# A conditioned decoder trunk on one core: which of w_ada's first groups are cut in two, in which order they load, and how the input projection begins

## What is computed

```python
sc = silu(c)                                  # 1 prompt row and 8 sampled rows
mod = sc @ w_ada + b_ada                      # w_ada (1024, 6144)
sh1, s1, g1, sh2, s2, g2 = split(mod, 6)
h = rmsnorm(x, norm1_g) * (1 + s1) + sh1      # shift sh1, scale s1
z = h @ w_in                                  # w_in (1024, 6144)
# z feeds three mixers (convolution, pooling, short convolution), gates, and w_o;
# then x + g1 * mixed, a second norm with sh2 and s2, 16 experts of which 2 serve a token, a last norm
```

## Time and profile before

| | before |
|---|---|
| median of 3 runs | 872.23 us |
| lowest, highest | 871.78, 873.41 us |
| profiled execution: span | 871.9 us |
| PE, PEld busy | 839.9, 701.3 us (96%, 80%) |
| DVE, ACT busy | 683.7, 465.4 us (78%, 53%) |
| chain that ended last | PE 82%, DVE 8%, DMA 3%, ACT 2% |
| mean granted TensorE clock | 0.987 |

### The profile page before, as it was taken

The page is one execution under the profiler, slowest core; times in us unless marked ns, Lnnn a source line. Parts: engine busy times, 40 slices in busy tenths (PEclk is TensorE's granted clock), DMA queues, the critical chain, the costliest instruction groups (busy, mean ns, idle before and its releaser), DMA issues.

```text
span 871.9 us, 14906 instructions
## 1 busy us (share of the span) xinstructions
PE 839.9 (96%) x5047; PEld 701.3 (80%) x5047; DVE 683.7 (78%) x939; ACT 465.4 (53%) x556; POOL 76.7 (9%) x71
## 2 busy tenths in 40 slices
PE   7899999999999999999999989999999999999994
PEld 2489999989899999899777457888888888887851
DVE  0781638978798678499438889999989999899888
ACT  4652442343422221642222457888888888888852
POOL 0002000000000000230000002000100001003750
PEclk9989999999999999999999999999999999999998
DMA  9858535354543231123671479988895899999962
GB/s 328 277 174 290 194 127 169 121 169 150 159 154 108 89 96 50 42 87 123 211 276 74 170 252 398 400 327 310 316 400 217 317 398 400 400 400 397 366 197 98
DMA packets 90997, 201.24 MB, mean 231 GB/s; under 512 B 8792, under 2 KB 13400, under 8 KB 90918
## 3 DMA queue, kind: packets, MB, share of 16 engines
q1 hardware_dynamic: 78813, 165.25, 53.4%
q0 software_dynamic: 5136, 18.42, 5.9%
q10 hardware_dynamic: 7003, 16.95, 5.3%
HBM read 182.97 MB, written 18.35 MB: 231 GB/s over the span
## 4 chain that ended last, share of the span: by engine, by line
PE 82%; DVE 8%; DMA 3%; ACT 2%; issue 2%; SPq 1%; ACTq 1%; POOL 0%; POOLq 0%; DVEq 0%
PE ps L804 31%; PE ps L655 12%; PE ps L657 12%; PE ps L656 12%; PE ps L884 3%; DVE w_lo L1590 2%; PE ps L999 2%; DMA region_a<-in_x_prompt_dram 2%; PE ps L836 2%; PE ps L1121 1%; PE ps L683 1%; ACT w_hi L1146 1%; PE ps L684 1%; DMA region_b<-h_rows,slot_idx 1%; PE ps L1034 1%
## 5 line engine op out<-in xcount | busy, mean ns | idle before, releaser
L1590 DVE TENSOR_TENSOR w_lo<-raw,w_hi 128x1024 fp32r<-128x1024 f32 x202 | 241.6, 1225 | 100.1 <-ACT w_hi L1146 98.0
L1146 ACT ACTIVATE w_hi<-raw 128x1024 fp32r<-128x1024 f32 x202 | 207.8, 1056 | 198.2 <-PE ps L804 150.6
L655 PE MATMUL ps<-w_hi,hT_hi 128*128 128x512 f32 (+1 forms) x512 | 205.5, 401 | 3.6 <-DVE w_lo L1590 1.4
L657 PE MATMUL ps<-w_hi,hT_lo 128*128 128x512 f32 (+1 forms) x512 | 202.1, 395 | 0.0
L656 PE MATMUL ps<-w_lo,hT_hi 128*128 128x512 f32 (+1 forms) x512 | 201.5, 394 | 0.0
L804 PE MATMUL ps<-hT_hi,w_hi 128*128 128x260 f32 x768 | 156.6, 285 | 1.7 <-DVE w_lo L1590 0.9
L804 PE MATMUL ps<-hT_lo,w_hi 128*128 128x260 f32 x768 | 155.1, 283 | 0.0
L804 PE MATMUL ps<-hT_hi,w_lo 128*128 128x260 f32 x768 | 155.0, 283 | 0.0
L804 PEld LDWEIGHTS ps<-hT_hi,w_hi 128*128 128x128 f32 x768 | 119.1, 190 | 5.0 <-DVE w_lo L1590 3.9
L804 PEld LDWEIGHTS ps<-hT_lo,w_hi 128*128 128x128 f32 x768 | 119.5, 190 | 0.0
L804 PEld LDWEIGHTS ps<-hT_hi,w_lo 128*128 128x128 f32 x768 | 118.9, 189 | 0.0
(11 more groups left out here) (332 smaller groups left out, 840.3 us busy)
## 6 DMA issues: line engine op xcount, KB each, us to landing
raw<-in_exp_w_dram SPq DMA_DIRECT2D x96, 512.0 KB
region_a<-in_exp_w_dram SPq DMA_DIRECT2D x80, 512.0 KB
raw<-in_w_in_dram SPq DMA_DIRECT2D x48, 512.0 KB
raw<-in_w_ada_dram SPq DMA_DIRECT2D x30, 512.0 KB
expert_rows<-region_b ACTq DMA_DIRECT2D x17, 512.0 KB, 6.4
region_b<-in_exp_w_dram SPq DMA_DIRECT2D x16, 512.0 KB
region_b<-in_w_ada_dram SPq DMA_DIRECT2D x14, 512.0 KB, 9.0
expert_rows<-region_a POOLq DMA_DIRECT2D x8, 512.0 KB, 8.3
```

The lines of the kernel that those rows point to most:

```text
L655: pe.matmul(out, pairs[0], moving[0], start=start, stop=False)
L657: return pe.matmul(out, pairs[1], moving[0], start=False, stop=stop)
L1146: act.activation(w_hi[:, split_slot(n), :], place, ACT.Copy).then_inc(hi_done, 1)
L1590: return dve.tensor_tensor(out, whole, first.bitcast(F32), ALU.subtract)
```

## The change

The roles of w_ada's first four groups are exchanged: the shift groups 0 and 1 become the split ones and load first, the scale groups 2 and 3 the native ones, and they load behind x, the last four of their quarters behind the first two quarters of z group 0. PE no longer runs the natives first: it runs the eight split quarters, turns parameters and both shift groups, 16 identity transposes, and then sets native quarters between the blocks of x. z group 0 is cut into parts of one quarter and one tile: tiles 0 to 2 of quarter 0 come first, then two native quarters, tiles 0 to 2 of quarter 1, then tile 3 of both. On ACT all eight hi cuts stand ahead of the squares, and ACT multiplies two of x's four tiles by the norm itself, with a `scale` operand. On DVE the shift is finished before the norm. The core of the diff:

```diff
-ITEMS = [("a", g) for g in range(G_NAT, G_HEAD)] + [("z", 0), ("z", 1)]
+ITEMS = [("a", g) for g in range(G_SPLIT)] + [("z", 0), ("z", 1)]
...
 # SP
-            for h in range(6):
-                native(h)
+            for n in range(N_HEAD):
+                quarter(n)
             sp.dma_start(x_in[0:ND, 4, :], ...)
             for i in range(NP // P):
                 sp.dma_start(x_in[:, i, :], ...)
-            for h in range(6, 4 * G_NAT):
+            for h in range(4):
                 native(h)
-            for n in range(N_MIX):
-                if n == N_HEAD + 4:
+            for n in range(N_HEAD, N_MIX):
+                if n == N_HEAD + 2:
+                    for h in range(4, N_NAT):
+                        native(h)
+                elif n == N_HEAD + RAW:
                     for dst, src in state_loads:
...
-                elif n == N_HEAD + RAW:
-                    sp.wait_ge(ssq_ready, NTILE)
+                elif n == N_HEAD + RAW + 2:
+                    sp.wait_ge(hT_lo_done, KD + 2)
                     sp.wait_ge(turned, 2)
...
 # PE
+            pe.wait_ge(cT_split, 2)
+            for n in range(4):
+                ada_quarter(n, 4)
+            for n in range(4, 8):
+                ada_quarter(n, 7)
+            turn_params()
+            pe.wait_ge(fold_ready, 1)
+            turn_mod(0, 0, 0)
+            turn_mod(1, 0, 36).then_inc(modT_done, 1)
+            head_running(16)
+            native_quarter(0)
+            native_quarter(1)
+            pe.wait_ge(xn_ready, NTILE)
+            for p, b in ((0, 2), (1, 3), (2, 4)):
+                turn_x(p, b)
+            native_quarter(2)
+            native_quarter(3)
+            for k in range(3, KD):
+                if k >= 4:
+                    pe.wait_ge(xT_out, k - 3)
+                turn_x(k, X_BANK[k])
+            turn_sampled()
+            native_quarter(4)
+            turn_mod(2, 7, 0).then_inc(modT_done, 1)
+            native_quarter(5)
...
+            pe.wait_ge(xT_out, KD)
+            for m in range(3):
+                z_part(0, 0, m)
+            native_quarter(6)
+            native_quarter(7)
+            z_part(0, 1, 0)
+            turn_mod(3, 6, 0).then_inc(modT_done, 1)
+            z_part(0, 1, 1)
+            z_part(0, 1, 2)
+            for q in range(2):
+                z_part(0, q, 3)
+            for q in range(2, 4):
                 for m in range(4):
+                    z_part(0, q, m)
...
 # ACT
-            native_out(0)
+            for n in range(N_HEAD):
+                hi(n)
             for n, i in enumerate((4, 0, 1, 2, 3)):
...
+            for i in (2, 3):
+                act.wait_ge(x_rooted, 1)
+                act.activation(x_in[:, i, :], x_in[:, i, :], ACT.Copy, scale=sums[:, 3, i:i + 1]).then_inc(xn_ready, 1)
+            for k in range(3):
+                turned_x(k)
+            hi(8)
+            hi(9)
+            native_out(0)
+            for k in range(3, KD):
+                turned_x(k)
+            input_sampled(0)
             for k in range(4):
-                turned_x(k)
+                input_prompt(k)
+            hi(10)
+            hi(11)
             native_out(1)
...
 # DVE
+            for n in range(4):
+                lo(n)
+            lo(4)
+            mod_group(0)
+            for n in range(5, N_HEAD):
+                lo(n)
+            mod_group(1)
+            params_out()
+            shift_out()
             mean_squares()
             norm_root()
-            for t in range(NTILE):
+            dve.wait_ge(shift_done, 2)
+            dve.sem_inc(x_rooted, 1)
+            for t in (4, 0, 1):
                 dve.tensor_scalar(x_in[0:rows(t), t, :], ..., None, ALU.mult).then_inc(xn_ready, 1)
```

More of the change, by code:

```diff
@@ L64 @@
 ITEMS += [("z", _g) for _g in range(2 + G_ADA - G_GAP - G_HEAD, G_IN)]
-A_AT = {g: ITEMS.index(("a", g)) for g in range(G_NAT, G_ADA - G_GAP)}
+A_AT = {g: i for i, (kind, g) in enumerate(ITEMS) if kind == "a"}
+SPLIT_GROUPS = [g for kind, g in ITEMS if kind == "a"]
+N_NAT = 4 * (G_HEAD - G_SPLIT)
 Z_AT = [ITEMS.index(("z", g)) for g in range(G_IN)]
-N_HEAD = 4 * (G_HEAD - G_NAT)
+N_HEAD = 4 * G_SPLIT
 N_MIX = 4 * len(ITEMS)
@@ L77 @@
 NR = NG + NE
+X_BANK = (2, 3, 4, 1, 2, 3, 4, 1)
 END_EARLY = (0, 4)
@@ L280, in trunk_step @@
         ld_x = sem("ld_x")
+        x_rooted = sem("x_rooted")
+        shift_done = sem("shift_done")
         x_landed = [sem(f"x_landed{i}") for i in range(NTILE)]
-        nat_ready = [sem(f"nat_ready{h}") for h in range(4 * G_NAT)]
+        nat_ready = [sem(f"nat_ready{h}") for h in range(N_NAT)]
         apart_ready = [sem(f"apart_ready{n}") for n in range(N_APART)]
@@ L781, in z_quarter @@
                 hi, lo = split_weights(n, 2)
-                for m in range(4):
[L783 to L806, removed]
@@ L808, in z_quarter @@
-                mm.then_inc(quarter_used, 1)
-            for i in range(G_HEAD - G_NAT, len(ITEMS)):
+                ms = slice(m * P, (m + 1) * P)
+                if q == 0:
+                    pe.wait_ge(set_free[m], g + 1)
+                    if m == 2 and g and ITEMS[n // 4 - 1][0] == "a":
+                        pe.wait_ge(mod_ready, SPLIT_GROUPS.index(ITEMS[n // 4 - 1][1]) + 1)
+                    elif m == 3 and g == 0:
+                        pe.wait_ge(scaleT_ready, 2)
+                for k in range(2):
+                    kk = 2 * q + k
+                    if g == 0 and m == 0:
+                        pe.wait_ge(hT_lo_done, kk + 2 + kk // 4)
+                    first, final = kk == 0, kk == KD - 1
+                    for w, x, start, stop in ((hi, hT_hi, first, False), (hi, hT_lo, False, False), (lo, hT_hi, False, final)):
+                        for h in range(2):
+                            mm = pe.matmul(ps[:, 2 * m + h, 0:HT], w[:, k, ms], x[:, kk, h * HT:(h + 1) * HT], start=start, stop=stop)
@@ new lines, in z_part @@
+                if m == 3:
+                    mm.then_inc(quarter_used, 1)
+                elif q == 3:
+                    mm.then_inc(z_done, 1)
+            pe.wait_ge(xT_out, KD)
[9 more added lines that the diff above has]
+                z_part(0, q, 3)
@@ L811, in _ @@
+            for q in range(2, 4):
+                for m in range(4):
+                    z_part(0, q, m)
+            for i in range(G_SPLIT + 1, len(ITEMS)):
                 kind, g = ITEMS[i]
@@ L820, in _ @@
                     else:
-                        z_quarter(g, q)
+                        for m in range(4):
+                            z_part(g, q, m)
             unit = [0]
@@ L1173, in turned_x @@
                 act.wait_ge(xT_done, k + 1)
-                act.activation(xnT[:, k, :], ps[:, k % 4, :], ACT.Copy).then_inc(xT_out, 1)
+                act.activation(xnT[:, k, :], ps[:, X_BANK[k], :], ACT.Copy).then_inc(xT_out, 1)
             def input_sampled(half):
@@ L1225, in _ @@
             act.wait_ge(pads_ready, 1)
-            for i in range(G_HEAD - G_NAT, len(ITEMS)):
+            for i in range(G_SPLIT, len(ITEMS)):
                 kind, g = ITEMS[i]
@@ L1648, in row @@
                     return pT[:, :, r + half:r + half + 1].broadcast_to([P, KW, ND + 1])
[L1650 to L1654, removed]
+                turned_scale = ps[:, 7, 0:36] if half == 0 else ps[:, 6, 0:36]
                 link(dve.tensor_tensor(scaleT[:, ks, :], turned_scale.rearrange("p (k s) -> p k s", s=9), row(R_BIAS + 2), ALU.add))
@@ L1696, in _ @@
             prompt_rest(0)
[L1697 to L1701, removed]
+            for k in range(1, 4):
                 prompt_sum(k)
                 prompt_rest(k)
-            lo(9)
+            lo(10)
             scale_out(1)
```

114 lines of the change are left out of this document (36 added, 78 removed).

## The result

The changed kernel takes 875.9 us (median of 18 runs, 872.4 to 881.6), the kernel before 872.37 (18 runs). The ratio is 1.0027, 95% interval 1.0015 to 1.0038: slower by 2.4 us by the ratio, where 3.2 less was forecast and 874.2 was the top of the range. The profiled execution took 876.63 with a span of 874.9, so 1.7 us lie around the span; the forecast for the span was 868.7.

A forecast was written before the change was run, and what follows sets the result against it. PE bounds the kernel from the projection on: start 4.15 earlier, cheaper pairs 2.3, plain turning 0.7, against 3.46 of native work and 0.5 of wait, gives 3.2 less: span 868.7, median 869.0 us, range 867.2 to 874.2.

The forecast's parts named there:

- Prices and landings: Head: work priced from profile rows, such as 1.73 us per native quarter; large loads land 1.36 us apart in issue order.
- PE as the chain from 24 on, natives on the path: Head: PE itself is the chain, native 1 ending at 29.7, 0.4 us beyond x's norm; projection starts at 42.2.
- Waits in z group 0: First group: a 0.5 us wait for block 1; second half's scale ready about 53, last lo block of x near 59.
- The clock, rival B: Head, 22 to 42 us: a short 1.2 GHz spell on PE's chain costs 2.3, giving 871.3; chance 0.22.
- working on transposes: Head, 21.9 to 26.3: if transposes do not count as PE-busy, PE gets no credit and natives start at 1.2 GHz.
- The step that failed: Handover to z group 1: 6.73 us as before, so it starts at 70.5 instead of 73.74; nothing differs behind it.
- that mark: Start of quarter 3 of z group 0: forecast at 63.8 us, against 67.01 in the kernel before.
- Rival D: Behind z group 0: later loads of ada group 4 and bias rows take the gain back, 872.2; chance 0.05.
- PE's clock as a risk of the head alone: Low clock considered only between 22 and 42 us; the main forecast keeps it up from about 20, chance 0.50.

The follow-up runs named there:

- a_hold_a4: Changed kernel, with SP holding the four loads of ada group 4 back until z group 0 has ended; 871.3 us, ratio 0.9976 to the kernel before.
- a_small_early: Changed kernel, with ACT's seven small transfers moved from behind hi(14) to between hi(11) and the last scale group's copy; 871.6 us, ratio 0.9974 to the kernel before.
- a_head0: Changed kernel without the 16 identity transposes ahead of native quarter 0; 874.3 us, ratio 1.0006 to the kernel before.
- a_nat6: Changed kernel with native quarter 6 ahead of the projection's first parts rather than behind them; 873.9 us, ratio 0.9993 to the kernel before.
- a_early_nat67: Changed kernel with the seven small transfers behind hi(11) and native quarters 6 and 7 ahead of the projection; 870.5 us, ratio 0.9962 to the kernel before.
- b_small_early: Kernel before, with the seven small transfers moved to between hi(9) and the second half's sampled rows; 872.7 us, ratio 0.9992 to the unmoved kernel before.
- a_early_nat6: Changed kernel with the seven small transfers behind hi(11) and native quarter 6 ahead of the projection; 870.4 us, ratio 0.9944 to the kernel before.

## Why the prediction was wrong

- **Prices and landings.** Right. Split quarters, natives, turnings and squares cost what their rows said (the five squares 6.1 us instead of 6.26), and a_hold_a4's profile follows the drawn times within 0.8 us up to quarter 3.
- **PE as the chain from 24 on, natives on the path.** Right: the first x turning follows native quarter 1 without a wait (27.30 + 4.13 = 31.43).
- **Waits in z group 0.** Idle 1.1 before the first L804 and 0.3 behind block 0, where 1.0 and 0.5 were expected. The second half's scale came at 54.95, not 53, since its copy waits for native 7, which ended at 52.94; in a_hold_a4, without the low clock, native 7 ended 1.9 earlier and the scale came at 53.06. The last block's rest ended at 62.3 instead of near 59: 1.9 of this is the same delay, and 1.2 a lo cut of weights (57.57) that DVE makes between blocks 4 and 5 and that the sum left out. SP's loads wait for this end.
- **The clock, rival B.** The low spell came in the forecast place. The prediction's working on transposes there takes in too much: of its 21.9 to 26.3 the two folded groups, 2.0 us, are matmuls with `fold` (L746), not transposes. In the profile it took 1.7 from the head (transposes 1.0 and natives 0.7 too long), less than B's 2.3, and even with B's whole price the sum would have been 871.3. Not in each execution: the runs' mean clocks go from 0.986 (881.6 us) to 0.994 (872.4).
- **The step that failed:** "z group 1 starts 6.73 behind that mark (the router and state loads that ACT issues, then its copy): 73.74 -> 70.5. Behind it nothing differs." The 6.73 was carried over as a constant; it measured 9.17, and z group 1 behind it took 24.79, not 23.27. It is a race: before, group 4's loads were issued from 60.05, 7.2 us ahead of ACT's first small issue (67.28), and in 68 to 70 the DMA engines moved 75 GB/s; after, SP waits for the last rest of x (62.3) and issues them from 62.8, 4.0 ahead of it (66.75), and in 68 to 70 they move 389 GB/s. The lead is 4 us without the low clock as well, since both ends moved with PE. Now ACT's small issues stand in the midst of them and cost 4.7 instead of 2.3 us for the two one-row loads. a_hold_a4 and a_small_early each end this, and give 4.5 and 4.6 us. Some 1.0 of it is the wait before z group 1 that the kernel before had too and that the forecast kept within its 6.73. By the marks the step was 2.4 + 1.5 = 4.0 us too small, of the 6.6 between forecast and profile; the other 2.7 are the low clock (1.7) and the small delays above (1.0).
- **Rival D** named the right transfers, and asked only for their own reader, 30 us away. It didn't ask who else was in the DMA engines at that time.
- **The half clock behind PE's idle time at 72 to 75.7** (1.5 us in z group 1) was in no case: the sum had PE's clock as a risk of the head alone.

## What to carry over

A stretch copied over from the profile as "the same length behind the mark" is a constant only if both of its ends move together: for each transfer that it issues, ask what will be in the DMA engines at its new time. Behind each wait that the change adds on a queue, list who shares the engines with what is held back, not only who reads it. Small transfers of no urgency belong where the work behind them on the issuing engine has to wait for something else anyway: here 4.6 us, more than the whole change was to bring, though their issue cost no less at the new place (5.1 us for the two one-row loads, 4.7 at the old).

## What the runs showed of the hardware

- Issuing a transfer of 2 KB that is spread over 128 partitions took ACT's queue 0.59 us with SP's loads held back (a_hold_a4), 0.70 in the kernel before, 2.69 to 3.04 in the midst of four 512 KB loads (a_head0, a_nat6, changed), 3.75 in a_small_early, 5.25 in a_early_nat67, and 5.26 in b_small_early, beside the last loads of z group 1 and the state rows:

```profile
44.93 5.26 ACTq L1210 DMA_DIRECT2D rbias<-in_router_g_b_dram  x1
45.26 1.51 ACT L1185 ACTIVATE hT_hi<-region_b,shiftT,scaleT 128x512 fp32r<-128x512 f32 x2
```

  The second row shows copies that stand ahead of the transfers in the program and run while the queue is already issuing. What stands behind the transfers starts only after the last issue, at 53.25 here and at 74.91 in the changed kernel (last issue 74.16 + 0.65).
- PE idle from about 72.3 to 75.66 (PEclk 1.00 all through) went to half clock from about 76.2 to 79.7. The idle time that the rows give just before z group 1, and the length of z group 1: 3.22 us and 24.79 (changed), 3.16 and 26.01 (a_nat6), 1.62 and 23.26 (a_head0), 0.83 and 23.27 (before); the first two ran at half clock for a while, the last two did not. Each is one execution.
- The kernel before has two levels of its own. Of the 69 runs of it beside the experiments, 30 with a mean granted clock of 0.991 or more have a median of 871.9 us, 38 with 0.989 or less 875.1. The changed kernel's runs spread over the same clocks in no such groups. Ratios to the kernel before therefore carry up to some 0.2% that is its own clock's doing: beside the changed kernel its median was 872.37, near the first level, beside a_early_nat6 874.73, near the second.
